# The tail of a one-core decoder step in another order: last residual, last choices, sample rows, and the first gather ahead of most weights

## The chip, the cores and the metric

The kernel runs on one core of a Trainium2 chip. The time is the device time of one execution, in microseconds (us); of the kernel before there are three timed runs, 1411.78, 1413.25 and 1415.09 us, with a median of 1413.25 us. One more execution was profiled: 1411.79 us, of which the recorded span is 1409.9 us. The engines have queues of their own and meet through semaphores only: PE (matmuls), DVE (elementwise work and reductions), ACT (activations), POOL (here mostly issuing of gathers) and SP (here only issuing of transfers).

## The reference

One layer for 1024 prompt tokens and 32 sample tokens (8 sequences of 4 new tokens), in float32. Attention and the recurrent mixer are not touched. What matters here is the end of the layer: the output projection with its residual, the second norm, the choice of experts, and the experts.

```python
x = x + mixed @ w_out[l]
x = x + hier_moe(rmsnorm(x, norm2_w[l]), ...)
...
def hier_moe(h, wg, bg, we, be, w1, w3, w2):
    t = h.reshape(-1, shp[-1])
    pg = jax.nn.softmax((t @ wg) + bg, axis=-1)              # 4 groups
    p_top, g_idx = lax.top_k(pg, 1)
    le = ((t @ we) + be).reshape(-1, N_GROUPS, EXPERTS_PER_GROUP)
    le_sel = jnp.take_along_axis(le, g_idx[:, :, None], axis=1)[:, 0]
    top_l, e_idx = lax.top_k(le_sel, 2)                      # 2 of 4 experts
    gate = p_top * jax.nn.softmax(top_l, axis=-1)
    ...
    for e in range(N_EXPERTS):                               # 16
        he = jax.nn.silu(t @ w1[e]) * (t @ w3[e])            # 1024 -> 256
        y = y + combine[:, e:e + 1] * (he @ w2[e])           # 256 -> 1024
```

The results are the normed rows of both passes and the keys, values and states of the layer.

## The kernel before, in words

The 1056 tokens are nine tiles: tiles 0 to 7 hold 128 prompt tokens each, tile 8 the 32 sample tokens. Sample attention reads pages of the cache all along the way (`decode`, spread over "spots").

*Output projection and router.* Tiles 0 to 7 are worked through in quarters `(i, q)`. On PE a quarter is `mixed_out` (L1372: 8 matmuls of 512 columns of the first or second half of the sum over k, for one half of the output), and between the quarters of tile i stand three steps for tile i - 1: `flip` (L1391, eight transposes of the normed rows), `router` (L1403, the logits, 32 rows at a time) and `router_sum` (L1408, which adds the four partial rows). DVE adds the residual (`residual`, L1905), inverts the norm (`norm2`: L1586 and L1592 to L1595), takes the flipped rows from the banks (`keep_flipped`, L1929), adds the router's bias (`logits`, L1940), and then chooses (`choose`, L1953 to L1973): the best group, the two best experts in it, their one-hot rows and a running sum of them. ACT squares the rows (`mean_square`, L959 and L961), scales them (`normed`, L971) and copies the router's partial rows out of the bank (`keep_logits`, L965).

*Sample rows.* Their attention output is normed in steps that the semaphore `d_step` counts: ACT squares (L982, L988), DVE forms the mean (L1586), ACT takes the root (L991), DVE inverts and scales (L1592 to L1595, L2009, L2010), PE transposes (L1460), DVE takes them over (L2016), and PE multiplies them by the output weights (`sample_out`, L1381, in two halves). Then come their residual (`sample_residual`, L1909), the square (L995), the sum over partitions on PE (`sample_square`, L1413), mean, root and inverse (`sample_mean` L1919, L997, `sample_norm` L1592 to L1595), the scaling (L1000), transposes (`sample_flip`, L1420; `sample_keep`, L1934) and logits (`sample_router`, L1427).

*Routing.* When the last tile is chosen, `routing` reaches "counts". PE sums the one-hot rows (L1472 to L1475), DVE gives every (token, choice) a slot in tiles of 160 rows of one expert (L2038 to L2060), PE turns the slots round into the row numbers of each tile (L1482), ACT copies them (L1008), PE adds them (L1486, L1487), and DVE writes them as integers to `ids` (L2074, L2075). Before that DVE has written which expert each tile has (`eid`, L2066 to L2071).

*Experts.* For each of the tiles, in pairs of slots s = 0, 1, POOL copies two columns of `ids` into `idx_cur` (L703) and issues two indirect transfers, of 128 and of 32 rows of 4 KB (L706, L708), from the rows' copy in memory. SP issues the weights of the tile's expert: w1 (L563), w3 (L564) and w2 (L567), 1 MB each, and in the loop the refills (L601, L603, L605), each as soon as PE has read the weights before it. PE transposes the gathered rows (`flip_rows`, L1498, L1500) and multiplies: `hidden` (L1513, 64 matmuls; w1 is read by the first 32 of them and w3 by the last 32), and `down` (L1528, L1533). Each engine's order is the order in which its program is written; there is no scheduler.

The waits ahead of the first gather and the first weights:

```python
pool.wait_ge(sem("routing"), ROUTING["ids"])          # POOL, then gather(0, 0), gather(0, 1)
sp.wait_ge(sem("routing"), ROUTING["experts"])        # SP, then expert_in(0), expert_in(1), expert_down(0), expert_down(1)
```

## Time and profile before

| | |
|---|---|
| median of three runs | 1413.25 us (1411.78 to 1415.09) |
| profiled execution | 1411.79 us, span 1409.9 us |
| PE busy | 1256.0 us, 89% of the span |
| DVE, ACT, POOL busy | 625.7, 367.4, 122.1 us |
| chain that ended last | PE 73%, DVE 12%, SP's queue 4%, issue 4%, ACT 3%, DMA 3% |
| output projection, last quarter starts | 1069.2 us |
| last choice is made | 1094.4 us |
| first gathered rows are there | 1118.9 us |
| first 64 matmuls of the experts start | 1123.8 us |
| end of the experts' work on PE | 1369.7 us |

Busy time is the time in which an engine worked on an instruction; the chain follows the last instruction back to what released it, step by step, so that its shares sum to the span. "Idle before" in a row is how long the engine had nothing to do ahead of that instruction, and what ended it. PEclk is the clock that was granted to PE as a share of the full one: 0.50 is 1.2 GHz and 1.00 is 2.4 GHz.

### The profile page before, as it was taken

The numbers are of one execution on the slowest core, as the hardware profiler recorded it, in microseconds if no ns is written. First come the engines' busy times: TensorE is split into PE (matmuls) and PEld (weight loads), VectorE is DVE, ScalarE is ACT, GpSimd is POOL, SyncE is SP. The second block draws the span as 40 slices with busy tenths as digits, with TensorE's granted clock in tenths as the row PEclk, the third lists the DMA queues.
The fourth block names the chain that finished last, engine by engine and source line by source line (L and its number), as shares of the span: only waits on it lengthen the run. The fifth ranks groups of instructions, "written<-read, shape, count | busy, mean of one in ns | idle before, by whom it ended". The sixth has DMA issues, their size and how long they took to land.

```text
span 1409.9 us, 24200 instructions
## 1 busy us (share of the span) xinstructions
PE 1256.0 (89%) x9261; PEld 894.9 (63%) x9261; DVE 625.7 (44%) x1464; ACT 367.4 (26%) x756; POOL 122.1 (9%) x288
## 2 busy tenths in 40 slices
PE   6999997989999899988787878998997399999987
PEld 5666885667678788765455545544453388887852
DVE  4001315435364645556967776475525412112117
ACT  4020201212222224334554645222122011111113
POOL 4400000000000002021000010100000111111013
PEclk9999998999999999999898999999998599999998
DMA  7811001010020206569897888999980599999838
GB/s 244 300 53 31 30 30 45 31 32 30 3 90 0 63 0 226 168 239 328 300 327 247 296 300 314 311 363 326 324 294 20 184 308 301 295 308 299 280 113 319
DMA packets 158308, 274.03 MB, mean 194 GB/s; under 512 B 13448, under 2 KB 72752, under 8 KB 158208
## 3 DMA queue, kind: packets, MB, share of 16 engines
q1 hardware_dynamic: 139776, 217.46, 45.9%
q0 software_dynamic: 11648, 38.39, 7.8%
q10 hardware_dynamic: 6784, 16.85, 3.4%
q8 instruction: 64, 1.05, 0.3%
q14 instruction: 36, 0.29, 0.1%
HBM read 235.55 MB, written 37.09 MB: 193 GB/s over the span
## 4 chain that ended last, share of the span: by engine, by line
PE 73%; DVE 12%; SPq 4%; issue 4%; ACT 3%; DMA 3%; POOL 0%; DVEq 0%; ACTq 0%; POOLq 0%
PE bank L1089 16%; PE bank L1092 13%; PE bank L1513 10%; PE bank L1372 5%; DVE arena L1791 4%; PE bank L1533 4%; PE bank L1138 4%; SPq L558 3%; PE bank L1258 3%; PE bank L1217 3%; PE bank L1324 2%; PE bank L1066 1%; PE bank L1302 1%; PE bank L1528 1%; DVE arena L1855 1%
## 5 line engine op out<-in xcount | busy, mean ns | idle before, releaser
L1089 PE MATMUL bank<-arena 128*128 128x352 f32 x768 | 240.5, 473 | 0.0
L1089 PEld LDWEIGHTS bank<-arena 128*128 128x128 f32 x768 | 148.3, 196 | 81.1 <-issue 7.7
L1092 PE MATMUL bank<-arena 128*128 128x256 f32 (+1 forms) x864 | 195.7, 384 | 0.6 <-issue 0.6
L1092 PEld LDWEIGHTS bank<-arena 128*128 128x128 f32 (+1 forms) x864 | 155.6, 183 | 32.7 <-issue 5.5
L1791 DVE STREAM_TRANSPOSE arena<-arena 128x512 f32<-128x512 f32 x256 | 156.1, 674 | 23.0 <-DMA arena<-in_cache_k_dram 22.8
L1513 PEld LDWEIGHTS bank<-arena 128*128 128x128 f32 x1024 | 143.2, 193 | 9.2 <-issue 9.2
L1513 PE MATMUL bank<-arena 128*128 128x160 f32 x1024 | 144.2, 303 | 1.9 <-DVE arena L2103 1.9
L1372 PE MATMUL bank<-arena 128*128 128x512 f32 x256 | 117.8, 603 | 0.9 <-ACT arena L914 0.9
L1217 PE MATMUL bank<-arena,tab 128*32 128x256 f32 x1024 | 69.2, 416 | 30.0 <-DVE arena L1791 20.3
L770 ACT ACTIVATE arena<-bank 128x352 f32<-128x352 f32 x48 | 22.2, 463 | 234.9 <-PE bank L1089 234.9
L1372 PEld LDWEIGHTS bank<-arena 128*128 128x128 f32 x256 | 46.4, 191 | 52.9 <-issue 52.8
L1217 PEld LDWEIGHTS bank<-arena,tab 128*32 128x32 f32 x1024 | 34.0, 118 | 63.3 <-issue 36.1
L1258 PE MATMUL bank<-arena 128*32 128x128 f32 x2048 | 66.2, 275 | 3.4 <-DMA arena<-in_cache_v_dram 2.8
L1258 PEld LDWEIGHTS bank<-arena 128*32 128x32 f32 x2048 | 53.3, 110 | 22.5 <-issue 21.1
L2108 DVE TENSOR_TENSOR arena<-arena,bank 128x320 f32<-128x320 f32 x16 | 7.8, 488 | 130.9 <-PE bank L1513 130.9
L904 ACT ACTIVATE arena<-arena,small 128x128 f32<-128x128 f32 (+7 forms) x64 | 48.7, 764 | 45.9 <-DVE small L1855 45.8
L1533 PE MATMUL bank<-arena 128*128 128x512 f32 x128 | 59.2, 606 | 0.0
L1138 PEld LDWEIGHTS bank<-arena 128*128 128x128 f32 x448 | 54.4, 192 | 4.3 <-issue 0.4
L1138 PE MATMUL bank<-arena 128*128 128x128 f32 x448 | 54.6, 276 | 0.0
L1717 DVE COPY_PREDICATED arena<-tab,bank 128x512 f32<-128x512 int32 x56 | 37.4, 723 | 36.0 <-PE bank L1142 36.0
L1302 PE MATMUL bank<-arena 64*128 64x512 f32 (+3 forms) x192 | 50.5, 574 | 1.7 <-DVE small L1855 1.6
L670 POOL COPY tab<-arena 32x16 f32<-32x16 f32 x128 | 25.7, 200 | 246.6 <-PE bank L1227 239.4
(342 smaller groups left out, 1488.6 us busy)
## 6 DMA issues: line engine op xcount, KB each, us to landing
arena<-in_cache_k_dram SPq DMA_DIRECT2D x256, 256.0 KB, 4.8
arena<-in_cache_v_dram SPq DMA_DIRECT2D x256, 256.0 KB, 3.8
arena<-in_expert_w_dram SPq DMA_DIRECT2D x48, 1024.0 KB, 7.5
arena<-in_w_in_dram SPq DMA_DIRECT2D x14, 1024.0 KB, 5.0
expert_scratch<-route POOLq DMA_DIRECT2D x40, 256.0 KB, 6.9
expert_scratch<-arena ACTq DMA_DIRECT2D x16, 512.0 KB
out_dram<-arena SPq DMA_DIRECT2D x12, 512.0 KB, 3.0
arena<-in_x_prompt_dram SPq DMA_DIRECT2D x4, 1024.0 KB, 9.4
```

Of the source, the lines that this page charges most:

```text
L558: sp.dma_start(ring4[s4][r:P:4, :].rearrange("p (i d) -> p i d", i=4), src.rearrange("(i b) d -> b i d", b=32)).then_inc(sem(f"pages{s4}") ...
L904: nc.scalar.activation(zp[n % 2][:, sl], zp[n % 2][:, sl], ACT.Exp, scale=-1.0, bias=a[:, m:m + 1], accum_out=a[:, 2 + m:3 + m]).then_inc( ...
L1089: mm = nc.tensor.matmul(bank(g)[:, 0:N3], w[:, k, c * P:(c + 1) * P], hT[:, k * TOK + n * N3:k * TOK + (n + 1) * N3], start=(k == 0), stop ...
L1092: mm = nc.tensor.matmul(bank(g)[0:ROWS[c], 0:256], tok(hT, k, c), w[:, k, :], start=(k == 0), stop=(k == KC - 1))
L1138: mm = nc.tensor.matmul(ps[bb + c // 4][:, (c % 4) * P:(c % 4 + 1) * P], a, b_, start=True, stop=True)
L1217: mm = nc.tensor.matmul(ps[5][32 * h:32 * h + 32, 0:256], q[:, c * 32:(c + 1) * 32], k8[:, :, c, :], start=(j == 0), stop=(j == 3))
L1258: mm = nc.tensor.matmul(ps[7][32 * h:32 * h + 32, 0:P], lhs, ring4[q4 % QUADS][:, i * HW + h * P:i * HW + (h + 1) * P], start=(g == 0 and ...
L1302: nc.tensor.matmul(ps[k % 3][:, 0:w], qT[rows, h * TOK + i * P:h * TOK + (i + 1) * P], kT[rows, h * TOK + j * P:h * TOK + j * P + w], star ...
L1372: mm = nc.tensor.matmul(ps[n][:, :], tok(mix_da if kk < H else mix_hg, kk % H, i), wout[k][:, n * 512:(n + 1) * 512], start=(k == 0), stop ...
L1513: mm = nc.tensor.matmul(ps[3 + m // 2][:, (m % 2) * TR:(m % 2 + 1) * TR], w13[:, k, m * P:(m + 1) * P], xT[s][:, k * TR:(k + 1) * TR], sta ...
L1533: mm = nc.tensor.matmul(ps[5 + n][:, :], he[s][:, k * TR:k * TR + P], w2[:, k * D + n * 512:k * D + (n + 1) * 512], start=(k == 0), stop=( ...
L1791: V.transpose(page, page).then_inc(sem("k_flip"), 1)
```

## The change

Line numbers above are those of before; after the change they are shifted by up to 30. What it does:

1. PE: `router(6)` stands ahead of the last quarter's `mixed_out(7, 3)` instead of behind it; the eight transposes of the sample rows stand ahead of `router_sum(6)`; `router_sum(7)` stands ahead of `sample_flip`.
2. ACT: the root of the sample norm (L991) stands ahead of `keep_logits(6)`; `keep_logits(7)` ahead of the wait for the sample rows' norm and their scaling; the copy of the row numbers (L1008) ahead of the two exponentials of the gates.
3. DVE: `logits(6)` and the first half of `choose(6)` come ahead of `norm2(7)`, the second half behind it and ahead of `sample_residual`; `keep_flipped(7, 1)` ahead of `sample_mean`; `choose_group(7)` ahead of `sample_keep`. For tiles 7 and 8 three instructions of `choose` that only the gates or the slots need (L1954, L1962 and the second one-hot row, L1973) come later.
4. POOL and SP: the first two gathers read their numbers from `ids` itself and have no copy before them. SP issues w1 of slot 0, waits until the gathered rows of slot 0 are there, and only then issues the other five weight transfers, in the order w3, w2 of slot 0, then w1, w3, w2 of slot 1.

```diff
@@ SP
             def expert_in(s, e):
                 ...
                 sp.dma_start(w13[:, :, 0:FF], w1_v[...]).then_inc(sem(f"wexp{s}"), 16)
+                if s == 0:
+                    sp.wait_ge(sem("xg_in0"), 32)
                 sp.dma_start(w13[:, :, FF:2 * FF], w3_v[...]).then_inc(sem(f"wthr{s}"), 16)
             for s in range(2):
                 e = sp.value_load(eid[0:1, s:s + 1], min_val=0, max_val=NE - 1)
                 expert_in(s, e)
-            for s in range(2):
-                e = sp.value_load(eid[0:1, s:s + 1], min_val=0, max_val=NE - 1)
                 expert_down(s, e)
@@ POOL
+            def rows_in(s, idx):
                 pool.indirect_dma_start(out=xg[s], ..., ap=idx[:, 2 * s:2 * s + 1], ...)
                 pool.indirect_dma_start(out=xgs[s][0:TB, :], ..., ap=idx[0:TB, 2 * s + 1:2 * s + 2], ...)
-            gather(0, 0)
-            gather(0, 1)
+            pool.sem_inc(sem("seen"), 1)
+            rows_in(0, ids)
+            rows_in(1, ids)
@@ ACT
+                if (i, q) == (7, 3):
+                    act.wait_ge(sem("d_step"), 3)
+                    nc.scalar.activation(orms[0:16, :], oms[0:16, :], ACT.Sqrt).then_inc(sem("d_act"), 1)
                 if i and q == 3:
                     keep_logits(i - 1)
...
-                if (i, q) == (7, 3):
-                    act.wait_ge(sem("d_step"), 3)
-                    nc.scalar.activation(orms[0:16, :], oms[0:16, :], ACT.Sqrt).then_inc(sem("d_act"), 1)
...
             nc.scalar.activation(rstd[:, 8:9], ss[:, 8:9], ACT.Sqrt).then_inc(sem("rms1"), 1)
+            keep_logits(7)
             act.wait_ge(sem("rstd1"), TILES)
             ...
-            keep_logits(7)
+            act.wait_ge(sem("routing_ps"), 3)
+            nc.scalar.activation(quarter_ids, ps[5][:, 0:TR], ACT.Copy).then_inc(sem("routing_act"), 1)
             act.wait_ge(sem("routing"), ROUTING["group"])
             nc.scalar.activation(gexp, gexp, ACT.Exp).then_inc(sem("routing_act"), 1)
...
-            act.wait_ge(sem("routing_ps"), 3)
-            nc.scalar.activation(quarter_ids, ps[5][:, 0:TR], ACT.Copy).then_inc(sem("routing_act"), 1)
@@ PE
+                if (i, q) == (7, 3):
+                    router(6)
                 mixed_out(i, q)
...
-                if i and q == 3:
+                if 0 < i < 7 and q == 3:
                     router(i - 1)
...
-            router_sum(6)
             pe.wait_ge(sem("d_step"), 4)
             ... eight transposes
+            router_sum(6)
...
             router(7)
+            router_sum(7)
             sample_flip()
-            router_sum(7)
             sample_router()
@@ DVE
-            norm2(7)
-            sample_residual()
-            logits(6)
-            choose(6)
-            keep_flipped(7, 0)
-            sample_mean()
-            keep_flipped(7, 1)
+            logits(6)
+            choose_group(6)
+            norm2(7)
+            choose_experts(6)
+            sample_residual()
+            keep_flipped(7, 0)
+            keep_flipped(7, 1)
+            sample_mean()
             sample_norm()
             logits(7)
+            choose_group(7)
             sample_keep()
-            choose(7)
+            choose_experts(7)
             logits(8)
             choose(8)
-            dve.sem_inc(sem("routing"), 1)
-            V.tensor_tensor(gate2.unsqueeze(2), v3[:, :, 1:2], v3[:, :, 0:1], ALU.subtract).then_inc(sem("routing"), 1)
+            second(7)
+            second(8)
@@ DVE, behind the write of ids
+            for i in (7, 8):
+                group_terms(i)
+            ch.wait()
+            dve.sem_inc(sem("routing"), 1)
+            for i in (7, 8):
+                expert_terms(i)
+            ch.wait()
+            V.tensor_tensor(gate2.unsqueeze(2), v3[:, :, 1:2], v3[:, :, 0:1], ALU.subtract).then_inc(sem("routing"), 1)
```

On PE, around the last quarter, the program before had these rows (L1454 and L1381: combination and first half of the sample projection; L1372: the last quarter; L1403, L1408: router and sum of tile 6; L1460: the transposes).

```order
L1454 MATMUL bank<-arena,small 16x128
L1381 MATMUL bank<-arena 32x256 x16
L1372 MATMUL bank<-arena 128x512 x4
L1403 MATMUL bank<-arena,wr 32x128 x8
L1408 MATMUL bank<-tab,arena 128x32
L1460 MATMUL bank<-tab,arena 128x16 x8
L1381 MATMUL bank<-arena 32x256 x16
```

Now the same place reads (L1408 is now the router, L1377 the last quarter, L1466 the transposes, L1413 the sum, L1386 the sample projection):

```order
L1461 MATMUL bank<-arena,small 16x128
L1386 MATMUL bank<-arena 32x256 x16
L1408 MATMUL bank<-arena,wr 32x128 x8
L1377 MATMUL bank<-arena 128x512 x4
L1466 MATMUL bank<-tab,arena 128x16 x8
L1413 MATMUL bank<-tab,arena 128x32
L1386 MATMUL bank<-arena 32x256 x16
```

The router has moved ahead of the last quarter, and the sum behind the transposes.

On DVE, behind the last residual, the program before went on with the norm of tile 7 (L1586 to L1595), the sample residual (L1909), and only then the logits and the choice of tile 6 (L1940 and on).

```order
L1905 TENSOR_TENSOR arena<-bank,arena 128x512
L2016 TENSOR_SCALAR arena<-bank,small 128x4x32
L1586 TENSOR_SCALAR small<-small 128x1
L1592 RECIPROCAL small<-small 128x1
L1593 TENSOR_TENSOR small<-small 128x1
L1594 SCALAR_TENSOR_TENSOR small<-small 128x1
L1595 SCALAR_TENSOR_TENSOR small<-small 128x1
L1909 TENSOR_TENSOR arena<-bank,arena 128x256
L1940 TENSOR_TENSOR route<-bank,small 128x24
L1953 MAX route<-route 128x8
```

Now the logits (L1947) and the choice of the group (L1970 to L1976) of tile 6 stand between, ahead of the norm (L1593 and on).

```order
L1912 TENSOR_TENSOR arena<-bank,arena 128x512
L2044 TENSOR_SCALAR arena<-bank,small 128x4x32
L1947 TENSOR_TENSOR route<-bank,small 128x24
L1970 MAX route<-route 128x8
L1957 TENSOR_SCALAR route<-route 128x4
L1973 MAX_INDEX route<-route 128x8
L1974 CAST route<-route 128x1
L1976 TENSOR_SCALAR arena<-tab,route 128x4
L1593 TENSOR_SCALAR small<-small 128x1
L1599 RECIPROCAL small<-small 128x1
```

Six instructions have moved from behind the sample residual to ahead of the norm; the sample residual now follows the rest of tile 6's choice.

On SP, the first weights before (two of the transfers of 128x8x256 a slot, then the two of 128x2x1024; each slot's number is loaded twice):

```order
L563 DMA arena<-in_expert_w_dram 128x8x256
L564 DMA arena<-in_expert_w_dram 128x8x256
L589 TENSOR_LOAD route
L589 ISA x2
L563 ISA
L563 DMA arena<-in_expert_w_dram 128x8x256
L564 DMA arena<-in_expert_w_dram 128x8x256
```

And now, with the wait for the gathered rows between the first two (an order shows no waits):

```order
L564 DMA arena<-in_expert_w_dram 128x8x256
L567 DMA arena<-in_expert_w_dram 128x8x256
L570 ISA
L570 DMA arena<-in_expert_w_dram 128x2x1024
L592 TENSOR_LOAD route
L592 ISA x2
L564 ISA
```

The transfer of w2 of slot 0 (L570) has moved ahead of both of slot 1.

## Rows read from the trace of the kernel before

**Rows 1.** The chain of waits, 1072 to 1145 us (start us, us, what):

```profile
1072.93 0.62 PE bank L1403 x16
...
1076.25 0.69 DVE arena L1905
...
1077.38 3.54 PE bank L1381 x32
...
1094.19 0.25 DVE arena L1969
...
1110.98 7.89 DMA arena<-rows_scratch,route
...
1123.82 11.36 PE bank L1513 x64
...
1141.30 8.69 PE bank L1513 x64
```

**Rows 2.** Timeline, 1067 to 1080 us (start, us, engine, line, operation, [idle before <-releaser]):

```profile
1068.00 0.16 DVE L1586 TENSOR_SCALAR small<-small 16x8 f32<-16x8 f32 x1 [0.91 <-ACT arena L988]
...
1073.97 0.19 DVE L1592 RECIPROCAL small<-small 16x8 f32<-16x8 f32 x1 [5.81 <-ACT small L991]
...
1078.48 0.15 DVE L1586 TENSOR_SCALAR small<-small 128x1 f32<-128x1 f32 x1 [1.22 <-ACT small L961]
...
1079.38 1.15 ACT L971 ACTIVATE arena<-arena,small 128x1024 f32<-128x1024 f32 x1 [0.93 <-DVEq L1915]
```

**Rows 3.** Timeline, 1080 to 1095 us:

```profile
1080.94 0.42 DVE L1909 TENSOR_TENSOR arena<-bank,arena 128x256 f32<-128x256 f32 x1 [1.66 <-PE bank L1381]
1081.29 0.17 DVE L1940 TENSOR_TENSOR route<-bank,small 128x24 f32<-128x24 f32 x1
...
1082.29 0.23 DVE L1958 TENSOR_SCALAR arena<-tab,route 128x4 f32<-128x4 f32 x1
...
1084.30 0.69 DVE L1929 TENSOR_TENSOR arena<-bank,small 128x512 f32<-128x512 f32 x1
...
1085.14 0.20 ACT L997 ACTIVATE small<-small 128x1 f32<-128x1 f32 x1 [3.23 <-DVEq L1920]
...
1085.94 1.08 PE L1403 MATMUL bank<-arena,wr 128*32 128x128 f32 x16 [3.73 <-DVE arena L1929]
...
1088.19 0.18 DVE L1940 TENSOR_TENSOR route<-bank,small 128x24 f32<-128x24 f32 x1 [1.65 <-PE bank L1408]
...
1088.82 0.23 DVE L1954 TENSOR_SCALAR route<-route 128x4 f32<-128x4 f32 x1
1088.95 0.09 DVE L1955 MATCH_VALUE_LOAD route<-route 128x8 f32 x1
```

**Rows 4.** Timeline, 1107 to 1136 us:

```profile
1107.92 0.41 SPq L563 DMA_DIRECT2D arena<-in_expert_w_dram  x1
...
1108.58 0.18 POOL L703 COPY route<-arena 128x2 int32<-128x2 int32 x1 [20.41 <-DVEq L2076]
...
1109.66 1.02 POOL L706 DMA_INDIRECT arena<-rows_scratch,route  x1 [0.90 <-POOL route L703]
...
1130.95 1.28 ACT L1019 ACT_TABLE_LOAD   x1 [18.26 <-PE bank L1513]
```

**Rows 5.** Windows (PE, PEld, DVE, ACT, POOL busy, PEclk, DMA share, GB/s):

```profile
1109.50:1119.00 9.50, 0.00 (x0) 0.03 (x1) 0.32 (x2) 2.74 (x9) 3.94 (x5) 0.50 1.04 342
...
1123.80:1128.70 4.90, 4.88 (x18) 4.88 (x19) 0.00 (x0) 0.00 (x0) 1.18 (x2) 0.50 1.05 387
...
1140.00:1355.00 215.00, 215.00 (x1509) 176.46 (x1508) 39.89 (x71) 29.47 (x51) 24.25 (x36) 1.00 0.87 281
```

**Rows 6.** From issue to landing, line L708 (32 rows), whole span:

```profile
DMA to landing us min/median/max: 3.7/5.3/8.5
```

**Rows 7.** From issue to landing, lines L563 (w1) and L564 (w3), 1100 to 1130 us:

```profile
DMA to landing us min/median/max: 5.4/9.7/14.0
...
DMA to landing us min/median/max: 10.6/13.9/17.1
```

More of the change, by code:

```diff
@@ L296, in build @@
         lgall = rt(TILES * RW)
-        g8, gi, e8, ei = rt(8), rt(8, U32), rt(8), rt(8, U32)
+        gi, ei = rt(8, U32), rt(8, U32)
+        g8, e8 = [rt(8) for _ in range(3)], [rt(8) for _ in range(3)]
         gidx, v12, i12 = rt(TILES), rt(TILES * 2), rt(TILES * 2)
@@ L300, in build @@
         gexp = rt(TILES * 4)
-        slotf, slot_i, row_i, row_j = rt(2 * TILES), rt(2 * TILES, I32), rt(2 * TILES, I32), rt(2 * TILES, I32)
-        cnt_i, ntl, endt, base = rt(NE, I32), rt(NE), rt(NE), rt(NE)
+        slotf, slot_i, row_j = rt(2 * TILES), rt(2 * TILES, I32), rt(2 * TILES, I32)
+        ntl, endt, base = rt(NE), rt(NE), rt(NE)
         eid_f, eid = rt(CAP), rt(CAP, I32)
@@ L469, in build @@
         NV_TOTAL = 16 * 9
-        ROUTING = {"counts": 1, "group": 2, "pair": 3, "slots": 4, "experts": 6, "ids": 7, "gates": 8}
+        ROUTING = {"counts": 1, "slots": 2, "experts": 4, "ids": 5, "group": 6, "pair": 7, "gates": 8}
         GATHERED = [("knat_out0", 48), ("knat_out1", 32), ("knat_out2", 32), ("knat_out3", 32), ("zeros_out", 32 * (2 * PAIRS - SURE) * TR // P)] + [(f"yg{i}", 0) for i in range(5, TILES)]
@@ L702, in gather @@
                 n = t * 2 + s
[L703 removed]
+                nc.gpsimd.tensor_copy(idx_cur[:, 2 * s:2 * s + 2], ids[:, ds(n * 2 + 4, 2)]).then_inc(sem("idx"), 1)
                 pool.wait_ge(sem("idx"), n + 1)
                 pool.sem_inc(sem("seen"), 1)
+                rows_in(s, idx_cur)
+            def rows_in(s, idx):
                 pool.indirect_dma_start(out=xg[s], out_offset=None, in_=rows_d,
[L707 removed]
+                                        in_offset=bass.IndirectOffsetOnAxis(ap=idx[:, 2 * s:2 * s + 1], axis=0)).then_inc(sem(f"xg_in{s}"), 16)
                 pool.indirect_dma_start(out=xgs[s][0:TB, :], out_offset=None, in_=rows_d,
[L709 to L712 removed]
+                                        in_offset=bass.IndirectOffsetOnAxis(ap=idx[0:TB, 2 * s + 1:2 * s + 2], axis=0)).then_inc(sem(f"xg_in{s}"), 16)
+            pool.sem_inc(sem("seen"), 1)
+            rows_in(0, ids)
+            rows_in(1, ids)
             turns = pool.value_load(more_i[0:1, 0:1], min_val=1, max_val=PAIRS - 1)
@@ L716, in _ @@
                     pool.wait_ge(sem("xgT_ps"), t * 2 + s + 1)
-                    gather(t + 1, s)
+                    gather(t, s)
             pool.wait_ge(sem("ye_out0"), turns * 32 + 64)
@@ L1947, in _, with group_terms, expert_terms, second @@
             step(V.memset(ids, 0))
-            def choose(i):
+            def group_terms(i):
+                ch.step(V.tensor_scalar(gexp[:, i * 4:(i + 1) * 4], lgall[:, i * RW:i * RW + NG], g8[max(i - 6, 0)][:, 0:1], None, ALU.subtract))
+            def expert_terms(i):
+                ch.step(V.tensor_copy(v12[:, 2 * i:2 * i + 2], e8[max(i - 6, 0)][:, 0:2]))
+            def second(i):
+                ch.step(V.tensor_scalar(o2[:, i, :], cst("iota")[:, 0:NE], i12[:, 2 * i + 1:2 * i + 2], None, ALU.is_equal))
+            def choose_group(i):
                 dve.wait_ge(sem("lg"), i + 1)
                 lgi = lgall[:, i * RW:(i + 1) * RW]
-                step(V.max(g8, lgi[:, 0:8]))
-                ch.step(V.tensor_scalar(gexp[:, i * 4:(i + 1) * 4], lgi[:, 0:NG], g8[:, 0:1], None, ALU.subtract))
-                step(V.max_index(gi, g8, lgi[:, 0:8]))
+                gv = g8[max(i - 6, 0)]
+                step(V.max(gv, lgi[:, 0:8]))
+                if i < 7:
+                    group_terms(i)
+                step(V.max_index(gi, gv, lgi[:, 0:8]))
                 step(V.tensor_copy(gidx[:, i:i + 1], gi[:, 0:1]))
                 step(V.tensor_scalar(off[:, i, :], cst("iota")[:, 0:NG], gidx[:, i:i + 1], NEG, ALU.not_equal, ALU.mult))
+            def choose_experts(i):
+                lgi = lgall[:, i * RW:(i + 1) * RW]
+                ev = e8[max(i - 6, 0)]
                 lmi = lm[:, i * 16:(i + 1) * 16].rearrange("p (g e) -> p g e", e=EG)
                 step(V.tensor_tensor(lmi, lgi[:, 8:RW].rearrange("p (g e) -> p g e", e=EG), off[:, i, :].unsqueeze(2).broadcast_to([P, NG, EG]), ALU.add))
-                step(V.max(e8, lm[:, i * 16:(i + 1) * 16]))
-                ch.step(V.tensor_copy(v12[:, 2 * i:2 * i + 2], e8[:, 0:2]))
-                step(V.max_index(ei, e8, lm[:, i * 16:(i + 1) * 16]))
+                step(V.max(ev, lm[:, i * 16:(i + 1) * 16]))
+                if i < 7:
+                    expert_terms(i)
+                step(V.max_index(ei, ev, lm[:, i * 16:(i + 1) * 16]))
                 step(V.tensor_copy(i12[:, 2 * i:2 * i + 2], ei[:, 0:2]))
@@ L1972, in choose @@
                     ch.step(V.tensor_tensor(c3[:, i + 1, :], c3[:, i, :], M3[:, i, :], ALU.add))
-                ch.step(V.tensor_scalar(o2[:, i, :], cst("iota")[:, 0:NE], i12[:, 2 * i + 1:2 * i + 2], None, ALU.is_equal))
+                if i < 7:
+                    second(i)
+            def choose(i):
+                choose_group(i)
+                choose_experts(i)
             dve.wait_ge(sem("rw"), 64)
```

11 lines of the change are left out of this document (5 added, 6 removed).

## Prediction

> **What bounds the kernel now.** I read the chain of waits first, then the timeline around each of its long pieces, then windows for the clock and the transfers. From about 1140 to 1355 us PE is busy all the time at the full clock, while the transfers take 0.87 of their engines [rows 5]; nothing in the change touches that loop's work, so whatever comes out ahead of it moves the end by as much. Ahead of it the chain leaves PE. From 1076.25 us, the last residual, to 1094.44, the end of the last choice, it runs on DVE with three handshakes between [rows 1 to 3]; then come the routing steps on PE and DVE, and then one wait of 7.89 us for gathered rows [rows 1]. In that wait PE does nothing, and the transfer engines are full at 342 GB/s [rows 5]: the gather shares them with weights that nobody needs yet.
>
> **Part 1, the sample norm and the last residual.** DVE stands 5.81 us for the root L991 [rows 2]. The root needs only the mean, which was there at 1068.16 [rows 2]; it is late because ACT has the copy of tile 6's logits ahead of it, and that waits for the router, which PE does only behind the last quarter, at 1072.93 [rows 1]. DVE is then in the inverse and scaling until 1076.2, and only then takes the last residual (1076.25), although PE had left its bank at 1072.93 [rows 1]. Now the root can run at about 1068.3, and the 2.3 us from 1073.97 to 1076.25 [rows 1, 2] end near 1070.6, under the last quarter. That quarter itself ends 0.62 us later, because the router stands ahead of it [rows 1]: 1073.55. So the residual starts at 1073.6, 2.65 us earlier than 1076.25. It is the next late thing: PE's quarter ends last now, not DVE.
>
> **Part 2, what fills DVE from there to the last choice.** Before, DVE spent 18.2 us from 1076.25 to 1094.44 [rows 1], of which it stood for 1.22 (root of tile 7), 1.66 (second half of the sample projection) and 1.65 us (router sum of tile 7) [rows 2, 3], 4.53 together. I place the new order with the old durations:
> - residual 0.7, the sample copy 0.35: 1074.65. Logits and group choice of tile 6 take 1.23 us (1081.29 to 1082.52 [rows 3]): 1075.9. Meanwhile ACT squares tile 7 as before, 1.5 us behind the residual, and its root is done at 1075.8 (1078.48 − 2.65 by [rows 2]). So the 1.22 us are gone.
> - norm of tile 7, 0.9 us (1078.48 to 1079.38 [rows 2]): 1076.85; the experts' half of tile 6's choice, 1.75 us (1082.55 to 1084.30 [rows 3]): 1078.6. The sample projection starts on PE at 1074.75 and takes 3.54 us at most [rows 1]: 1078.3, just ahead of the residual that needs it. The 1.66 us are gone too.
> - sample residual 0.42; two takings of flipped rows, 0.6 and 0.7; mean 0.2: 1080.45. Here the change opens a new gap: before, the second taking stood behind the mean and covered ACT's root L997 (0.20 us and two handovers of 0.05 to 0.1 [rows 3]). Uncovered that is 0.3 us. Inverse 0.75: 1081.5.
> - PE's router of tile 7 starts at 1080.35 and takes 1.08 us at 1.2 GHz [rows 3]; ACT's copy 0.3, PE's sum 0.45: 1082.3. DVE stands 0.8 us, where it stood 1.65.
> - logits and group 1.1, sample taking 0.4, the experts' half 1.5: 1085.35. The sample router (about 1.05 us) has ended at 1084.95. Choice of the samples: 2.8 us: 1088.15.
> The three instructions that leave each of the last two choices save less than they last, since the next one had started early: L1955 starts 0.13 us behind L1954's start, which lasts 0.23 [rows 3]. At 0.08 to 0.14 us each (the second one-hot row of tile 8 was already behind the end) that is 0.5 us, contained above. The later instructions lie beside PE's sums or behind `ids`. The sum of parts 1 and 2 is 1094.45 − 1088.15 = 6.3 us. Its bounds: if PE's sample work moves as little as the chain's first wait, 2.65 + 0.5 = 3.2 remain; if PE keeps the full clock, the router of tile 7 falls from 1.08 to 0.62 us [rows 1, 3] and 6.8 result. The steps are all measured and I stay at 6.3.
>
> **Part 3, routing.** The same 14 us. ACT copies the row numbers as before; the exponentials come behind it, with a table load of 1.28 us such as that of L1019 [rows 4] now in the open. It delays only the gates, which nothing reads before the rows come back from the experts, and ACT's next duty, the first SiLU, is 12 us behind the gather [rows 4]. Cost 0; with that cover gone it would be 1.3 us.
>
> **Part 4, the first gather.** Times here are on the old scale. The copy of the row numbers goes: 0.18 us of work and its handover; the 0.90 us between copy and gather [rows 4] I leave nearly whole, since a gather behind any wait needs its issue. I take 0.35 us. Then the contention. The gather's 0.655 MB landed at 1118.87 [rows 1]. w1 was issued at 1107.92 and landed 5.4 us later, at 1113.3 [rows 4, 7]. By then some 1.30 MB had moved, estimated from 342 GB/s over the 3.8 us since 1109.5 [rows 5]; 1.05 of it was w1. In the new order w1 and the gather are all there is, 1.70 MB: the missing 0.40 MB needs 1.2 us at that rate, and I add 0.2 since the gather ends alone: 1114.7. That saves 4.2 us in all. The bounds come from L708 over the whole span: its fastest landing, 3.7 us behind an issue at 1110.6, gives 1114.3 and 4.6 us; its median of 5.3 [rows 6], in the loop where weights always run, gives 1115.9 and 3.0 us. I stay at 4.2, nearer the row that has w1 alone in it.
>
> **The new wait.** Behind SP's wait stand five weight transfers and then the loop's refills. After the gather w3 of slot 0 is wanted first: the SiLU's releaser, the first 32 matmuls, ended at 1130.9 [rows 4], 12.0 us behind the landing. In the old order w3 took 10.6 us [rows 7] with the whole crowd around it; now only the second gather is ahead. Slack 1.4 us in the worst reading, 7 in the likely one. w1 of slot 1 is third in the queue, by 3.1 + 0.65 + 0.65 MB at 342 GB/s about 13 to 14 us behind the landing; it is wanted at 1141.3 [rows 1], 22.4 us behind. Cost 0.
>
> At the landing 1.6 MB more are still to be moved than before. The loop has 0.13 of its transfer capacity free [rows 5], so that is made up in some two rounds, and no weight is wanted sooner than about 20 us after its buffer is free.
>
> **The clock.** After the gather PE works at 0.50 until 1128.7, 4.9 us into the first 64 matmuls [rows 5]; they take 11.36 us instead of 8.69 [rows 1], 2.67 us for 4.9, so each us of shift of the rise is worth 0.55. I take the same distance. The Trainium skill ("TensorE: Matmul & The Clock Gate", Part 1: The HAM clock gate) says that the activity monitor runs free and isn't reset by the kernel; by that, where the rise falls among the matmuls is chance. No run here shows how far it moves; it would leave the sum as it is. From the rows, a rise at once would give 2.7 us back, and one that is 1.3 us later costs 0.7; I allow 0.7 either way.
>
> **Sum.** 6.3 + 4.2 = 10.5 us. The profiled execution's 1411.79 us becomes 1401.3 (the 1.89 us outside the span stay). That execution was 1.46 us below the median, so I predict 1413.25 − 10.5, about 1402.7 us.
>
> **Rivals.**
> A. Sharing, not crowding. Each transfer engine might serve POOL's and SP's queues by turns, so that five transfers less behind w1 change nothing as long as w1 is there; the gather's 7.89 us would be mostly its own scattered rows. Then part 4 gives the copy and a little, 1.0 us at most, the total is 7.3 and the time 1406.0. The Trainium skill says so of the turns ("DMA: Bandwidth & Descriptors", Queues, rings and completion order: engines go round the queues with work, packet by packet). The trace speaks against it: equal turns at 342 GB/s would have moved 0.655 MB in 3.8 us, and it took 7.89 [rows 1, 5], against a median of 5.3 [rows 6]. 7 in 100.
> B. The handshakes come back. If DVE, PE and ACT go in lock step in the new order (samples and tile 7 share ACT and bank), the tail gives only the 3.2 us of its lower bound, and the time is 1413.25 − 3.2 − 4.2 = 1405.9. For it: three engines in turn, with margins as small as 0.3 us. Against: each standing time has a named filler that is longer than it. 8 in 100.
> C. Slower: the weights held back become the bound. PE would stand in the first `hidden` for w3, from 12.0 us behind the gather on. Every us later is a us lost; at 10.6 us (old issue to landing) nothing is lost; the kernel is slower than before only from 22.5 us on, for example 1418.7 at 28. For it: the slack for w3 is the smallest of all. Against: the largest of all landings of w1 and w3 there was 17.1 us [rows 7], in a longer queue, and even that would cost only 5.1 (1407.8). 3 in 100, and 3 more for a loss in this place that brings the kernel back to no change.
> D. The sample work doesn't matter: the router of tile 7 hides the moved pieces, or the clock stays high from 1077 on, and the gain is 12 us or more: 1401 or less. 6 in 100.
>
> **How the numbers follow.** The forecast has 73 in 100: 1402.7 us, within about 2.5. The range 1399.0 to 1406.5 takes in A and B, the clock's 0.7 and the spread of the runs, and leaves out C and the far end of D. The measurement can't tell less than about 0.2% (2.8 us) from no change; A and B lie beyond that. Faster by more: 0.94; within: 0.03; slower: 0.03.
>
> **What would show it.** The root of the sample norm near 1068 us and the last residual near 1073.6; DVE without gaps from there but for two, of 0.3 and 0.8 us; the last choice near 1088.2. The gather's wait 3.7 to 4.5 us instead of 7.89. The second 32 matmuls of the first `hidden` without a wait. I am wrong if PE stands inside the first `hidden`, if the wait for the gather stays above 6 us, or if the last choice ends later than 1090.

## The result and the profile after

The changed kernel took 1399.32 us (median of four executions, 1397.17 to 1399.51), against 1412.76 us for the kernel before in the same comparison (four, 1411.78 to 1415.09): a ratio of 0.9899, with a 95% interval of 0.9882 to 0.9916. That is 11.9 to 16.7 us faster. The forecast was 10.5 us less, with a range that began at 1399.0 us; 0.9899 of the 1413.25 us that stood for the kernel before is 1398.98, just outside it. Two later measurements of the same pair, with more executions, gave 0.9932 (0.9907 to 0.9957) and 0.9927 (0.9910 to 0.9944), that is 9.6 and 10.3 us. Most of what follows is about that difference. One of the executions below, of the gather alone, took 1684.97 us at a granted clock of 0.735, in a slower state of the chip, and is left out.

The profiled execution after the change has a span of 1395.3 us, 14.6 less than before. The chain of waits after the change (start us, us, what), in the places of [rows 1]:

```profile
1061.84 0.52 PE bank L1408 x15
1062.36 3.64 PE bank L1377 x8
...
1066.03 0.69 DVE arena L1912
...
1080.38 0.24 DVE arena L1992
...
1095.62 1.02 POOL arena L710
...
1096.94 5.56 DMA arena<-rows_scratch,arena
...
1107.46 10.42 PE bank L1520 x64
...
1124.00 8.69 PE bank L1520 x64
```

A float32 matmul stands in the profile as two entries (a transpose as one): the last quarter's L1377 x8 is 4 matmuls of the program, and the experts' L1520 x64 is 32. Where the description of the kernel and the text below say 8 matmuls of a quarter or 64 of the experts, entries are meant.

The last residual (L1912) follows the last quarter (L1377) at once, the last choice (L1992) ends 14.6 us behind it instead of 18.2, and the wait for rows is 5.56 us instead of 7.89. The timeline (start, us, engine, line, operation, idle before) shows the steps that answer to [rows 2, 3]:

```profile
1060.88 0.21 ACT L990 ACTIVATE small<-small 16x8 f32<-16x8 f32 x1 [0.28 <-DVEq L2034]
...
1061.12 0.19 DVE L1599 RECIPROCAL small<-small 16x8 f32<-16x8 f32 x1 [0.33 <-ACT small L990]
...
1066.03 0.69 DVE L1912 TENSOR_TENSOR arena<-bank,arena 128x512 f32<-128x512 f32 x1 [2.77 <-PE bank L1377]
...
1072.76 0.97 PE L1408 MATMUL bank<-arena,wr 128*32 128x128 f32 x16 [0.41 <-DVE arena L1936]
...
1073.10 0.16 DVE L1599 RECIPROCAL small<-small 128x1 f32<-128x1 f32 x1 [0.33 <-ACT small L1002]
...
1074.79 0.18 DVE L1947 TENSOR_TENSOR route<-bank,small 128x24 f32<-128x24 f32 x1 [0.95 <-PE bank L1413]
```

The root (L990) no longer waits for the router, DVE's 5.81 us are 0.33, and the two gaps that were forecast are there, 0.33 and 0.95 us.

But those rows do not start where they should. The row from which both programs' tails can be counted is the combination of the sample heads on PE, just ahead of all that was changed. In the profile before:

```profile
1067.18 0.28 PE L1454 MATMUL bank<-arena,small 128*16 128x128 f32 x1
```

and after:

```profile
1059.81 0.28 PE L1461 MATMUL bank<-arena,small 128*16 128x128 f32 x1
```

So 7.4 of the 14.6 us had been gained before the first changed instruction ran. I therefore count in stretches from that row on, in every profile: to the sums of the one-hot rows (L1472 before), from there to the end of the row numbers' sums (L1487), PE's idle time up to the first transposes of gathered rows, and from these to the next tile's transposes, behind the first 64 matmuls of the experts. The rows of the sums and of the first transposes, before:

```profile
1094.54 0.61 PE L1472 MATMUL bank<-arena,ones 128*128 128x16 f32 x2 [4.73 <-DVEq L1970]
...
1119.00 1.94 PE L1498 MATMUL bank<-tab,arena 128*128 128x128 f32 x8 [10.95 <-DMA arena<-rows_scratch,route]
```

and after:

```profile
1080.72 0.61 PE L1479 MATMUL bank<-arena,ones 128*128 128x16 f32 x2 [3.26 <-DVEq L1993]
...
1102.64 1.94 PE L1505 MATMUL bank<-tab,arena 128*128 128x128 f32 x8 [8.40 <-DMA arena<-rows_scratch,arena]
```

In us:

| profile | combination starts at | to the sums | to the row numbers | PE idle | first tile | all four |
|---|---|---|---|---|---|---|
| before | 1067.18 | 27.36 | 13.51 | 10.95 | 16.02 | 67.84 |
| before, repeated | 1065.15 | 27.44 | 13.52 | 10.84 | 15.93 | 67.73 |
| changed | 1059.81 | 20.91 | 13.52 | 8.40 | 15.08 | 57.91 |
| changed, repeated | 1068.20 | 21.06 | 13.51 | 7.90 | 15.12 | 57.59 |
| changed, third time | 1069.29 | 20.47 | 13.52 | 9.49 | 15.53 | 59.01 |

In the part that the change touches it brings 8.7 to 10.3 us, 9.6 on average: 6.3 to 7.0 in the tail, 1.4 to 3.0 in the wait for rows and 0.4 to 0.9 in the first tile. Of the first pair the rest is 7.4 us ahead of it and 2.7 us given back behind it (from the next tile's transposes to the end 274.9 us before, 277.6 after; 275.2, 275.4 and 275.1 in the other three; what the one profile gave back stays open).

### The profile page after: what moved, and what is told of

It reads as the page before. It is cut to its first block, busy times and chain, and to the rows that moved or that the text cites. A ratio compares the mean times of both kernels' runs of the same rounds, so it can differ in the third digit from the quotient of the medians.

```text
span 1395.3 us, 24178 instructions
## 1 busy us (share of the span) xinstructions
PE 1248.9 (90%) x9261; PEld 889.4 (64%) x9261; DVE 625.6 (45%) x1464; ACT 367.4 (26%) x756; POOL 121.9 (9%) x286
## 4 chain that ended last, share of the span: by engine, by line
PE 71%; DVE 13%; SPq 5%; issue 4%; DMA 3%; ACT 3%; another core or an unknown queue 0%; POOL 0%; DVEq 0%; POOLq 0%; ACTq 0%
PE bank L1094 16%; PE bank L1097 13%; PE bank L1520 10%; PE bank L1377 5%; PE bank L1540 4%; DVE arena L1798 4%; PE bank L1143 4%; SPq L559 3%; PE bank L1263 3%; PE bank L1222 3%; PE bank L1329 2%; PE bank L1307 1%; PE bank L1535 1%; DMA arena<-in_x_prompt_dram 1%; PE bank L1505 1%
## 5 line engine op out<-in xcount | busy, mean ns | idle before, releaser
L1094 PE MATMUL bank<-arena 128*128 128x352 f32 x768 | 237.0, 467 | 0.0
L1520 PEld LDWEIGHTS bank<-arena 128*128 128x128 f32 x1024 | 142.2, 192 | 9.2 <-issue 9.2
L1520 PE MATMUL bank<-arena 128*128 128x160 f32 x1024 | 143.3, 301 | 1.9 <-DVE arena L2141 1.9
L1377 PE MATMUL bank<-arena 128*128 128x512 f32 x256 | 118.4, 605 | 0.9 <-ACT arena L919 0.9
L1377 PEld LDWEIGHTS bank<-arena 128*128 128x128 f32 x256 | 46.4, 191 | 53.2 <-issue 53.1
```

The source lines that it names most:

```text
L1094: mm = nc.tensor.matmul(bank(g)[:, 0:N3], w[:, k, c * P:(c + 1) * P], hT[:, k * TOK + n * N3:k * TOK + (n + 1) * N3], start=(k == 0), stop ...
L1377: mm = nc.tensor.matmul(ps[n][:, :], tok(mix_da if kk < H else mix_hg, kk % H, i), wout[k][:, n * 512:(n + 1) * 512], start=(k == 0), stop ...
L1520: mm = nc.tensor.matmul(ps[3 + m // 2][:, (m % 2) * TR:(m % 2 + 1) * TR], w13[:, k, m * P:(m + 1) * P], xT[s][:, k * TR:(k + 1) * TR], sta ...
```

## Experiments

The comparisons ran on several chips, each with executions of the kernel before beside it: their median is 1411.85 to 1414.39 us where there are more than one. Six kernels below (root alone, postponed instructions, the three of the rows, half of w1) have one timed execution each, 1400.93 to 1408.50 us, which tells nothing here; they are read from their profiles alone.

**The kernel before against itself.** No edit.

> The kernel before, unchanged, timed against itself. In the first pair of profiles the part ahead of the tail, which the change does not touch, was 7.4 us shorter after the change (the sample projection's first half began at 1067.4 before and 1060.1 us after). Theory 1, chance of the single execution (where the low stretches of TensorE's clock fall, how long the transfers take): the ratio is 1.000 within 0.2%, and in this profile the sample projection begins somewhere from 1058 to 1070 us, not at 1067.4. Theory 2, something in the changed program makes the early part shorter every time: here it begins at 1067.4 within 1 us, since the program is the old one.

Ratio 1.0011 (0.9994 to 1.0027); the 30 executions of the kernel before ran from 1405.19 to 1418.15 us. In this profile the combination started at:

```profile
1065.15 0.28 PE L1454 MATMUL bank<-arena,small 128*16 128x128 f32 x1
```

The same program is 2.0 us earlier there than in its first profile, more than the 1 us that theory 2 allowed; theory 1 stands.

**The changed kernel again, twice.** No edit.

> The changed kernel, unchanged, a second time. Theory 1 (only the tail, the gather and the clock behind it are worth something: 6.4 + 2.6 + 0.9 us by the first pair of profiles): 9 to 11 us faster than the kernel before. Theory 2 (the early part is shorter every time as well): 13 to 15 us faster, and the sample projection begins at 1060.1 within 1 us.

> The changed kernel once more. Before it two measurements of the same change stand apart: 13.4 us between the medians of four executions each, and 9.0 us between 9 and 30 executions. Theory 1, the change is worth 9 to 10 us (6.4 in the tail, 2.5 to 3 in the wait for rows, up to 1 from the clock) and the rest of the first figure was the early part of the few executions taken: again 8 to 11 us between the medians. Theory 2, the change is worth 13 and the second measurement was low: 12 us or more.

Medians 1403.06 against 1412.09 us (9.0 less, over 9 and 30 executions) and 1401.83 against 1411.85 us (10.0 less, over 6 and 13). All four executions of the first comparison lay at 1399.51 us or below; of these fifteen only three do. Why the four lay together at the low end stays open. The first profile of the two:

```profile
1068.20 0.28 PE L1461 MATMUL bank<-arena,small 128*16 128x128 f32 x1
```

The changed program starts its tail 1.0 us later here than the old one did in its first profile, and 8.4 us later than it had done itself. Theory 2 of both falls. Over all sixteen profiles of this study, all with the same instructions up to this row, it starts between 1059.81 and 1072.62 us, with a standard deviation of 3.4 us. PE's clock varies with it. Two profiles, windows of 1020 us (PE, PEld, DVE, ACT, POOL busy, PEclk, DMA share, GB/s), first with the combination at 1069.21 us:

```profile
30.00:1050.00 1020.00, 924.29 (x6957) 642.63 (x6956) 505.29 (x1147) 289.40 (x606) 59.03 (x192) 0.95 0.51 176
```

and one with it at 1062.06:

```profile
30.00:1050.00 1020.00, 921.90 (x7081) 639.80 (x7083) 506.85 (x1155) 293.36 (x612) 59.04 (x193) 0.97 0.52 177
```

Added up from the clock's record in the traces, the low level lasted 92.2 us between 30 and 1050 us in the first and 68.3 in the second, and over the sixteen profiles its length and the start of the tail go together with a correlation of 0.87, 0.37 us for each us. That is a correlation; no run changes the clock of the early part alone.

**Tail alone, gather alone.** Each half of the change by itself: the changed kernel with POOL's and SP's programs of before, and the kernel before with the new ones.

> The new order on PE, ACT and DVE alone; the first two gathers and the first weights as before (copies of the row numbers, no wait, six weight transfers ahead). If the tail's own path gives what the pair of profiles shows: 6.4 us faster than before, with the last choice 18.8 us behind the router of tile 6 instead of 25.2. If the shorter early part comes with the program rather than by chance, 10 to 11 us faster. Rival: the gather wait grows by what the tail gave, since the weights and gather do not depend on it: 0 to 2 us faster.

> The new gather and weight order alone (numbers read in place, SP's wait behind w1); PE, ACT and DVE as before. By the pair of profiles 2.6 us from the end of the row numbers to PE's first transposes, and up to 1 us more or less by where the clock rises: 2 to 4 us faster than before. By the prediction's part 4, 4.2 us. If the early part is shorter with this piece of the program, 6 to 8 us.

Tail alone: ratio 0.9949 (0.9930 to 0.9967), 1403.29 us; stretches 20.46, 13.52, 11.07, 15.87, in all 60.92 us, 6.9 below before. Gather alone: 0.9984 (0.9962 to 1.0005), 1409.46 us over eleven executions; 27.26, 13.51, 8.21, 15.79, in all 64.77, 3.0 below. The two add up to 9.9 us against 9.6 for both together. The times alone, with a standard deviation of some 3 us between executions, could not have told the gather's part from nothing. The rival that the gather's wait would grow by what the tail gave is refuted: 11.07 against 10.84 and 10.95.

**The root alone.** The kernel before with

```
-                if (i, q) == (7, 3):            # behind decode, behind keep_logits(6)
+                if (i, q) == (7, 3):            # ahead of keep_logits(6)
                     act.wait_ge(sem("d_step"), 3)
                     nc.scalar.activation(orms[0:16, :], oms[0:16, :], ACT.Sqrt)
```

> The kernel before with one change: ACT takes the root of the sample norm ahead of its copy of tile 6's logits; PE and DVE keep their order. Read from the profile, from the start of the last quarter (L1372) on: before, the last residual comes 7.0 us behind it and the last choice ends 25.2 us behind it. If the root is what held DVE: the residual comes 3.7 us behind it (when PE leaves the bank, 3.3 us sooner) and the last choice ends 21.8 to 22.5 us behind it, since DVE's three later waits stay. Rival: the wait passes on to the router and its copy, which stand ahead of the transposes on PE, and the last choice gains less than 2 us.

```profile
1063.13 0.21 ACT L985 ACTIVATE small<-small 16x8 f32<-16x8 f32 x1 [0.28 <-DVEq L2006]
...
1063.37 0.19 DVE L1592 RECIPROCAL small<-small 16x8 f32<-16x8 f32 x1 [0.33 <-ACT small L985]
...
1067.85 0.69 DVE L1905 TENSOR_TENSOR arena<-bank,arena 128x512 f32<-128x512 f32 x1 [2.34 <-PE bank L1372]
```

The last quarter started at 1064.11, so the residual is 3.74 us behind it instead of 7.02, 3.3 us sooner. The last choice ends 21.7 us behind it, 0.1 less than was expected, and the first stretch is 23.81 instead of 27.4 us: this one moved instruction brings 3.6 of the tail's 6.3 to 7.0 us. The router of tile 7 took 0.65 us here, at the full clock, and 1.08 before, so the 0.3 us gained behind the residual are the clock's. Its rival (less than 2) falls.

**The postponed instructions.** The changed kernel with group terms, expert terms and second one-hot row of tiles 7 and 8 back in the choices.

```
-                if i < 7:
-                    group_terms(i)
+                group_terms(i)            # likewise expert_terms(i) and second(i)
```

> The changed kernel with the three postponed instructions of the choices of tiles 7 and 8 (group terms, expert terms, second one-hot row) back in their old places in the choices. Read from the profile: from the last residual's start to the end of the last choice DVE takes 14.6 us in the changed kernel. If postponing them is worth the 0.5 us of the prediction, 15.1; if DVE's other engines hide them, 14.6 to 14.7.

From the residual to the sums 14.71 us, against 14.24 to 14.25 in the seven profiles of the new tail order that, like this one, had the router of tile 7 at the full clock (0.64 us; 0.97 to 1.08 at the low one, where the same stretch is 14.69 to 14.84). So postponing is worth 0.46 us by this one profile, as forecast, and the clock about as much again. The wait for rows, which this edit does not touch, was 4.71 us here; it matters for what follows.

**What holds the rows up.** Three kernels: the changed one without SP's wait; with w1 held back too; and with the second gather issued only when the first has landed.

```
# no wait                              # w1 held too
-    if s == 0:                             +    if s == 0:
-        sp.wait_ge(sem("xg_in0"), 32)      +        sp.wait_ge(sem("xg_in0"), 32)
                                                 sp.dma_start(... w1 ...)
# one gather, POOL
     rows_in(0, ids)
+    pool.wait_ge(sem("xg_in0"), 32)
     rows_in(1, ids)
```

> As the changed kernel, but without SP's wait: the numbers are read in place and the six weight transfers (now in the order w1, w3, w2 of slot 0, then of slot 1) are issued at once. If the held-back weights are what shortens the wait for rows: it is 7.5 to 8.2 us again, and PE's idle time ahead of its first transposes is 10.5 to 10.9 us, only the 0.2 to 0.3 us of the copy below the 10.85 to 11.08 of before. If reading in place is what matters (a gather that starts ahead of the third weight): 5.0 to 6.5 us.

> As the changed kernel, but w1 of slot 0 also waits for the gathered rows, so that nothing else is being transferred while they come. Read from the profile: the wait for rows, 5.06 to 5.56 us in the profiles of the changed kernel and of the gather part alone, against 7.77 to 7.98 with six transfers ahead. Theory 1, w1 alone still crowds the gather: the wait falls below 4.3 us. Theory 2, the rest is the gather's own (issue, scattered rows, landing): it stays above 4.8. Either way w1 is then late: it takes some 5 us from its issue and is wanted 5 us behind the rows, so PE stands 0.5 to 2 us ahead of the first 64 matmuls.

> As the changed kernel, but POOL issues the gather of slot 1 only when the rows of slot 0 are there. If the second gather takes transfer time from the first, the wait for rows falls from 5.06 to 5.56 us to below 4.7. If the two follow each other in their queue, it stays from 5.0 to 5.6, and nothing later changes, since the rows of slot 1 are wanted 15 us later.

The wait in the chain without SP's wait:

```profile
1099.35 7.59 DMA arena<-rows_scratch,arena
```

With w1 held too, and what came behind it:

```profile
1105.89 4.06 DMA arena<-rows_scratch,arena
...
1110.12 6.87 DMA arena<-in_expert_w_dram
1117.04 11.13 PE bank L1520 x64
```

And with the second gather held:

```profile
1109.51 4.77 DMA arena<-rows_scratch,arena
```

Reading in place without holding weights back leaves 7.59 us and an idle PE of 10.42 us. That is 0.4 to 0.5 below before, but the root alone, which still has the copy, had 10.27, so the difference is within the variation. What the copy itself took can be read more closely: from the end of the row numbers on PE to the gather's issue it is 1.37 us instead of 1.61, so it was worth 0.24. With six transfers around it the wait was 7.21 to 7.98 us in five profiles. With only w1 ahead it was 5.56, 5.06 and 6.66 us in the three profiles of the changed kernel, 5.37 in that of the gather alone and 4.71 in that of the postponed instructions, so holding the others back brings about 2. In the profile with 6.66 w1 itself took 7.7 us to land, and 5.4 in the one with 5.06; why is not shown. With no weights at all ahead the wait is 4.06: w1 costs the rows another 0.7 to 2.6 us. In those 4.06 us the transfers moved 214 GB/s and not the 342 of [rows 5], with the second gather already behind the first, so a wait remains that no order of the weights takes away. But then PE waits for w1 until 6.96 us behind the start of its transposes, 2.1 more than the 4.8 that transposes and copies take, and the sum is 58.80 us, no better than the changed kernel. The second gather's result, 4.77, shows nothing: with the second gather not held, the wait was 4.71 to 6.66.

**Half of w1 ahead.** The first four steps of k ahead of the gather, the other four behind it:

```
+    sp.dma_start(w13[:, 0:4, 0:FF], w1_v[ds(e * D, 512), :]...)
     sp.wait_ge(sem("xg_in0"), 32)
+    sp.dma_start(w13[:, 4:8, 0:FF], w1_v[ds(e * D + 512, 512), :]...)
```

> The changed kernel, with only the first half of w1 (the first 4 of 8 steps of k) ahead of the gather, and the second half behind it. With all of w1 ahead the wait for rows was 5.06 to 5.56 us, with none 4.06. If w1 crowds in proportion: 4.4 to 4.8. PE wants the second half about 5 us behind the rows, and 0.5 MB took no less than 3.7 us to land in the rows' own queue: PE stands 0 to 1 us inside the first 32 matmuls, and the sum is a wash. If it is less than 0.3 us, this is up to 0.7 us better than the changed kernel.

The wait was 4.06 us, as short as with nothing ahead, against 4.4 to 4.8 expected, so the crowding is not in proportion to the weights. The first tile took 16.52 us instead of 15.1 to 15.5. That is the clock's: the full level came 6.0 us behind the first of the 64 matmuls and not 3.0 to 3.9 as in the changed kernel, and PE did not stand inside them. All four stretches are 57.41 us, 0.2 below the best profile of the changed kernel: a wash.

**The clock behind the gather.** Five, nine, or seven and fifteen matmuls of 512 columns that write a bank nobody reads, while PE waits for rows (and, the seven, ahead of the row numbers):

```
+    for _ in range(9):
+        nc.tensor.matmul(ps[6][:, :], ident, x1[0][:, 0:512], start=True, stop=True)
     pe.wait_ge(sem("routing"), ROUTING["experts"])
```

> The changed kernel with nine matmuls of 512 columns added on PE behind the sums of the row numbers, while it waits for the rows; they write a bank that nobody reads, and leave all results as they are. At the low clock they take 0.86 us each, 7.7 us, inside the idle 7.9 to 8.4 us. If the clock's low level is what makes the first transposes and the first 64 matmuls slow (1.94 + 1.00 and 10.4 us; 0.87 + 0.61 and 8.69 in the loop), they fall to those values: 1.4 + 1.7, 3.1 us less from the rows' landing to the end of the first 64 matmuls. If it is their first pass through the code that makes them slow, or if transfers hold them, nothing changes. If the added matmuls run past the landing, up to 0.5 us is lost.

> The same with 7 such matmuls in the idle time ahead of the row numbers (L1482 of before) and 15 in the wait for rows. If the first seven bring the clock back by the time the row numbers come, the latter's second half takes 1.0 us instead of 1.97 and the two sums 0.5 instead of 0.9, and the 15 take 6.5 us at the full clock: 4 to 4.5 us less in all than the changed kernel. If the clock is still low when the 15 start, they last up to 12.9 us and the rows wait up to 4.5 us for PE: 0 to 3 us slower than the changed kernel.

> The changed kernel with five added matmuls of 512 columns on PE in the wait for rows, instead of nine. Nine took 10.7 us (four at the low clock at 1.7 us each, five at the full clock at 0.87) and ended 2.8 us behind the rows' landing, which cancelled what they brought. If the low clock is the cause of the slow start, five end at about the landing, 7.7 us behind their start, and from the landing to the end of the first 64 matmuls it takes 12.3 to 13 us instead of 15.4 to 15.8 (nine: 15.2). The whole kernel is then 2.5 to 3 us below the changed one and 12 to 13 us below the kernel before. If the level falls again in the 0.2 to 1 us between, or hasn't risen by the landing, 0 to 1.5 us.

With nine:

```profile
1097.79 10.72 PE bank L1497 x18
1108.51 0.87 PE bank L1507 x8
1109.38 0.62 PE bank L1509 x8
...
1111.88 8.96 PE bank L1522 x64
```

Transposes and matmuls run at about the loop's speed (0.87, 0.61 and 8.69 us), so it is the clock that makes the first tile slow, and not its first pass through the code: it took 12.32 us instead of 15.1. But a matmul of 512 columns takes 0.87 us at the full clock, and 1.7 at the low one, twice what I had counted, since I had taken each of the profile's two entries (nine matmuls are x18) for a matmul; and the nine ended 2.8 us behind the landing. All four stretches: 57.46 us. With five, which fit, the level rose at 1104.2 us and fell again at 1111.1, just ahead of the 64 matmuls:

```profile
1103.18 5.07 DMA arena<-rows_scratch,arena
1108.38 1.06 PE bank L1507 x8
...
1111.95 11.85 PE bank L1522 x64
```

so what the transposes gained (1.06 and 0.63 us instead of 1.94 and 1.00) the matmuls lost again: 57.13 us. Seven and fifteen cost 2.0 to 3.4 us in the sum (61.03 against the changed kernel's 57.59 to 59.01), since the fifteen took 13.1 us and not 6.5. The whole times agree: ratios 0.9941 with nine, 0.9930 with five and 0.9942 with seven and fifteen, all with intervals of 0.002 to either side, none to be told from the changed kernel's 0.9932 and 0.9927.

## Why the prediction was wrong

*What failed.* The term that was mis-sized is the one under "How the numbers follow": "the spread of the runs". Below 1402.7 the range reached to 1399.0, 3.7 us; the better bounds of the tail (0.5), of the gather (0.4) and of the clock (0.7) take 1.6 of them, so some 2 us were left for the spread, judged from three executions that lay within 3.3 us. Thirty executions of the same program lie within 13 us, with a standard deviation of 3.2, and the untouched part ahead of the tail alone varies by 12.8 us between profiles. By that deviation the difference of two medians of four is uncertain by about 2.8 us (an estimate). Four against four executions gave 13.4 us between the medians for a change whose own stretch gave 9.6, and 9.0 and 10.0 us in the two repetitions. So the whole time left the range not by more gain in the changed part, which gave less than forecast, but by the executions that were taken. I had also made the sum against one profile and moved it to the median by the 1.46 us between them, as if that were a fixed distance.

*The sample root and the last residual (part 1): right.* Forecast 2.65 us earlier; from the combination to the residual it is 9.07 us before and 6.22 after, 2.85. The experiment with the root alone shows that this wait was the largest piece: even with nothing else it brings 3.3 us at the residual.

*The new order on DVE (part 2): right.* Forecast 6.3 us with 6.8 for the full clock; measured 6.3 to 7.0 in three profiles. The gaps came out at 0.33 and 0.95 us for 0.3 and 0.8, and the removed instructions at 0.46 for 0.5. Rival B is refuted. Of rival D only the clock came true: the second half of the sample projection ran at the full clock (1.93 us instead of 3.54), and so in one of three profiles did the router. The projection did so in all thirteen profiles with the root moved, even where nothing else was, and in none of the other three; there PE had stood for 1.9 us ahead of the transposes, and the level fell as the projection began.

*Routing (part 3): right.* 13.51 us before and 13.52 after; the table load lies beside PE's sums.

*The gather (part 4): direction right, too large.* Forecast 4.2 us; PE's idle time fell from 10.84 to 10.95 us to 7.90 to 9.49, by 2.3 on average. The estimate from moved bytes was wrong in taking all of the wait for the share of w1 and rows at 342 GB/s: with no weights in flight the rows still take 4.06 us from the second issue to their landing, at 214 GB/s. With w1 that makes 4.7 to 6.7, and the forecast had 4.1. The lower bound, 3.0, was the better guess, and even that was above the mean. One of the signs of being wrong, a wait above 6 us, was there in one of the three profiles (6.66). Rival A, a gain of 1.0 or less, is refuted: holding back the transfers behind w1 took the wait from 7.59 to between 4.71 and 6.66 us. For that rival I had taken the turns of the queues, which the Trainium skill states ("DMA: Bandwidth & Descriptors", Queues, rings and completion order), to mean that transfers queued behind w1 do no harm. The runs refute this reading; whether the queues go by turns no run here shows.

*The new wait: right.* PE never stood inside the first 64 matmuls. Rival C did not come near: w3 was issued 0.1 us ahead of PE's first transposes and wanted 11 us later.

*The clock: left at 0, was 0.4 to 0.9 us.* In [rows 5] the level rose 4.9 us behind the first of the 64 matmuls, which took 11.36 us; after the change it rose about 3.0 us behind it and they took 10.42, and 10.87 in the third profile. Windows of the profile after (same columns as [rows 5]):

```profile
1107.46:1110.50 3.04, 3.04 (x11) 3.04 (x12) 0.00 (x0) 0.00 (x0) 1.12 (x2) 0.50 0.99 369
1110.50:1117.70 7.20, 7.20 (x54) 7.20 (x54) 0.00 (x0) 1.72 (x2) 0.00 (x0) 1.00 1.08 346
```

That was within the 0.7 us allowed or just outside. It isn't a steady gain of the change: with the postponed instructions put back the rise came 4.5 us behind the first of the 64 matmuls, and the first tile took 15.80 us, only 0.2 less than before. The errors of part 4 (1.9 too much) and of the clock and the tail (some 1.0 too little) cancel in part, which is why 10.5 is close to the 9.6 that the stretch shows; that is luck as much as insight.

## What to carry to other kernels

Before a forecast of 1% is compared with a time, find out how far the untouched part of the kernel moves between executions, and judge the change in a stretch that begins at its first changed instruction. An engine whose queue holds a short instruction behind a long wait is worth looking for first: one square root that stood behind a copy it had nothing to do with was about half of this change's gain in the tail. Holding back transfers that nobody needs yet shortens a gather, but the gather has a time of its own, and that is what must be measured before the gain is counted.

## What the runs showed of the hardware

- The wait for 160 gathered rows of 4 KB, from the second issue to the landing: 7.21 to 7.98 us with six transfers of 1 MB issued around it, 4.71 to 6.66 with one, 4.06 with half of one or none (one profile each), at 214 to 217 GB/s.
- A float32 matmul of 512 columns is two entries of the profile and took 0.87 us at the full clock and 1.7 at the low one.
- Added matmuls in a wait did bring the clock up. With nine, which ran on until the transposes, it stayed up over the 1.9 us in which PE waits for DVE's copies; with five, behind which PE stood for 1.5 us more, it fell again for 6.8 us. One profile each.
- The low stretches of the clock between 30 and 1050 us add up to between 68.3 and 92.2 us in profiles of the same instructions.
